# Two stacked transformer blocks on one core: the modulation weights multiplied in fp32 as they land, and a new order of the first weight units

## The reference

```python
mod = silu(c) @ w_ada + b_ada            # w_ada: 1024 x 6144
sh1, sc1, gt1, sh2, sc2, gt2 = split(mod, 6)
mod_c = silu(c_ctx) @ w_ada + b_ada      # the context's, first two parts used
h  = rmsnorm(x, g_norm1) * (1 + sc1) + sh1
hc = rmsnorm(ctx, g_norm1) * (1 + scc1) + shc1
cq, ckv, kpe, rq, rk, rv, rg = split_proj(h @ w_in)   # and the same of hc
```

## Time and profile before

| | us |
|---|---|
| median of 3 runs (lowest, highest) | 853.25 (853.14, 853.38) |
| span of the profiled execution | 852.2 |
| runs' median less that span | 1.05 |
| PE busy | 834.3 (98%) |
| DVE busy | 588.2 (69%) |
| ACT busy | 468.1 (55%) |
| read from HBM | 150.97 MB, 178 GB/s over the span |

### The profile page before, as it was taken

The page is one execution under the profiler, slowest core; times in us unless marked ns, Lnnn a source line. Parts: engine busy times, 40 slices in busy tenths (PEclk is TensorE's granted clock), DMA queues, the critical chain, the costliest instruction groups (busy, mean ns, idle before and its releaser), DMA issues. The chain is left out here.

```text
span 852.2 us, 12805 instructions
## 1 busy us (share of the span) xinstructions
PE 834.3 (98%) x4919; PEld 721.0 (85%) x4919; DVE 588.2 (69%) x917; ACT 468.1 (55%) x757; POOL 16.8 (2%) x24
## 2 busy tenths in 40 slices
PE   7999999999999999999999999999999999999997
PEld 5798888877899999987889977788977788888785
DVE  5885978787778777796767676577547655555444
ACT  6866364366366666563555684646545644444442
POOL 1001000000000000000000000010000000000000
PEclk9999999999999999999999999999999999999999
DMA  9973573165656666568758643244504666665541
GB/s 332 374 237 98 173 229 106 50 198 173 217 169 184 198 186 183 179 205 310 240 145 290 196 149 100 75 164 158 173 25 149 185 185 198 177 192 177 190 154 49
DMA packets 103667, 152.85 MB, mean 179 GB/s; under 512 B 6538, under 2 KB 55862, under 8 KB 103608
## 3 DMA queue, kind: packets, MB, share of 16 engines
q1 hardware_dynamic: 102296, 149.21, 54.5%
q10 hardware_dynamic: 1312, 2.83, 0.9%
HBM read 150.97 MB, written 1.05 MB: 178 GB/s over the span
## 5 line engine op out<-in xcount | busy, mean ns | idle before, releaser
L2087 DVE TENSOR_TENSOR w_lo<-raw,w_hi 128x1024 fp32r<-128x1024 f32 (+1 forms) x244 | 294.9, 1213 | 150.2 <-ACT w_hi L1521 149.4
L1521 ACT ACTIVATE w_hi<-raw 128x1024 fp32r<-128x1024 f32 (+1 forms) x244 | 254.5, 1050 | 201.2 <-PE bank L738 142.2
L736 PE MATMUL bank<-w_hi,hT_hi 128*128 128x512 f32 (+2 forms) x400 | 156.1, 390 | 1.3 <-DVE w_lo L2087 0.6
L738 PE MATMUL bank<-w_hi,hT_lo 128*128 128x512 f32 (+2 forms) x400 | 152.9, 382 | 0.0
L737 PE MATMUL bank<-w_lo,hT_hi 128*128 128x512 f32 (+2 forms) x400 | 152.6, 382 | 0.0
L839 PE MATMUL bank<-hT_hi,w_hi 128*128 128x256 f32 x512 | 145.0, 283 | 0.0
L840 PE MATMUL bank<-hT_lo,w_hi 128*128 128x256 f32 x512 | 144.9, 283 | 0.0
L841 PE MATMUL bank<-hT_hi,w_lo 128*128 128x256 f32 x512 | 144.9, 283 | 0.0
L840 PEld LDWEIGHTS bank<-hT_lo,w_hi 128*128 128x128 f32 x512 | 98.3, 192 | 0.0
L839 PEld LDWEIGHTS bank<-hT_hi,w_hi 128*128 128x128 f32 x512 | 98.3, 192 | 0.0
L841 PEld LDWEIGHTS bank<-hT_hi,w_lo 128*128 128x128 f32 x512 | 98.3, 192 | 0.0
(11 more groups left out here) (341 smaller groups left out, 1197.9 us busy)
## 6 DMA issues: line engine op xcount, KB each, us to landing
raw<-w_up_dram SPq DMA_DIRECT2D x132, 256.0 KB, 3.2
raw<-w_ada_dram SPq DMA_DIRECT2D x48, 512.0 KB, 4.7
raw<-w_down_dram SPq DMA_DIRECT2D x44, 512.0 KB, 4.1
raw<-w_in_dram SPq DMA_DIRECT2D x40, 512.0 KB, 4.6
raw<-w_gate_dram SPq DMA_DIRECT2D x44, 256.0 KB, 2.8
raw<-w_out_dram SPq DMA_DIRECT2D x16, 512.0 KB, 3.4
raw<-wk_x_dram SPq DMA_DIRECT2D x8, 512.0 KB, 4.7
raw<-wv_x_dram SPq DMA_DIRECT2D x8, 512.0 KB, 3.4
```

The costliest lines, as they stand in the source:

```text
L736: pe.matmul(o, xh, yh, start=first, stop=False, skip_group_check=skip)
L738: return pe.matmul(o, xl, yh, start=False, stop=last, skip_group_check=skip)
L1521: act.activation(unit_view(w_hi[n % NSPLIT], u), unit_view(raw[u % NRAW], u), ACT.Copy).then_inc(w_hi_ready, 1)
L2087: dve.tensor_tensor(unit_view(w_lo[n % NSPLIT], u), unit_view(raw[u % NRAW], u), unit_view(w_hi[n % NSPLIT], u).bitcast(F32), ALU.subtract ...
```

## The change

- The sixteen units of ada0 to ada3 are no longer split. PE multiplies them in plain fp32 straight from `raw` (`direct_unit`): `c_cols` holds silu(c) in column 0 and silu(c_ctx) in column 1 of 32 (the rest are zeros, written by POOL), and each unit is four matmuls of 256 columns, one for each K tile and half of the columns, each on another 32 columns of the array. The four partial sums lie at PSUM partitions 0, 32, 64 and 96; `sel_col` (four columns now) adds them in `ada_spread`, with two matmuls instead of four. `modrow` is half as wide.
- The chunks come in the order 0, 2, 1, 3, and cq0, rq0 and rq1 are loaded, split and multiplied among the units of ada1 (the new `EARLIER`). x is loaded after units 1 and 3, the context after the last unit of ada3.
- PE waits for the landing (`raw_landed`) instead of `unit_ready`; SP waits for `direct_used` or the filled bank. `by_dve` counts the units that DVE still does.
- Fillers: 24 instead of 17 at the start, 4 instead of 3 after a unit, 16 instead of 8 (now after ada1's first unit).
- ACT makes silu from the bank itself, and splits cq1 before it does pairs 2 and 3 of x.

```diff
-EARLIER = {"cq": (("cq", 0), ("rq", 0), ("rq", 1)),
-           "wout2_0": (("wv1", 0), ("wv1", 1)),
-           "wo0": (("wo0", 0), ("wo0", 1), ("wo1", 0))}
+EARLIER = {("ada1", 0): (("cq", 0),), ("ada1", 1): (("rq", 0),), ("ada1", 3): (("rq", 1),),
+           ("wout2_0", 0): (("wv1", 0), ("wv1", 1)),
+           ("wo0", 0): (("wo0", 0), ("wo0", 1), ("wo1", 0))}
-    ada(range(4))
+    ada((0, 2, 1, 3))
-BUSY = {"score": 8, "start": 17, "spread": 8, "ada": 3,  "ffnpre": 14, "gu0": 8}
+BUSY = {"score": 8, "start": 24, "spread": 16, "ada": 4, "ffnpre": 14, "gu0": 8}
...
+            def direct_unit(u):
+                name, k0, nk, cols, _ = units[u]
+                use = (name, 0)
+                pe.wait_ge(raw_landed[u % NRAW], landed[u])
+                w = unit_view(raw[u % NRAW], u).rearrange("p (k n) -> p k n", k=nk)
+                for kk in range(nk):
+                    for half in range(2):
+                        j = 32 * (2 * kk + half)
+                        ins = pe.matmul(ps(use)[j:j + 32, 0:TOK], c_cols[:, k0 + kk, :],
+                                        w[:, kk, half * TOK:(half + 1) * TOK],
+                                        start=u == first_unit[name], stop=u == last_unit[name])
+                if u == last_unit[name]:
+                    fill(ins, use)
+                else:
+                    ins.then_inc(direct_used, 1)
...
+            turn_vectors(0, 4)
+            for p, b in ((0, 0), (2, 1), (1, 6), (3, 7)):
+                claim((f"ada{p}", 0), b)
+            idle = ps(("ada3", 0))[:, 0:P]
+            keep_busy(idle, BUSY["start"])
+            pe.wait_ge(csilu_ready, 3)
+            for u in units_of["ada0"]:
+                direct_unit(u)
+                keep_busy(idle, BUSY["ada"])
+            turn_vectors(1, 5)
             pe.wait_ge(in_sel, 16)
+            ada_spread(0, 2)
+            for u in units_of["ada2"]:
+                direct_unit(u)
+                if u != last_unit["ada2"]:
+                    keep_busy(idle, BUSY["ada"])
+            turn("x1", None, range(2), (4, 5))
+            ada_spread(2, 3)
+            direct_unit(units_of["ada1"][0])
+            keep_busy(idle, BUSY["spread"])
...
+            next(cq)
+            for u in units_of["ada1"][1:3]:
+                direct_unit(u)
+            next(rq)
+            direct_unit(last_unit["ada1"])
+            next(rq)
+            turn("x1", None, range(2, 4), (4, 5))
+            ada_spread(1, 6)
+            for u in units_of["ada3"]:
+                direct_unit(u)
             ada_spread(3, 7)
...
-                    sp.wait_ge(unit_ready, u - NRAW + 1)
+                    v = u - NRAW
+                    if not direct[v]:
+                        sp.wait_ge(unit_ready, by_dve[v])
+                    elif v in ends:
+                        ready(sp, (units[v][0], 0))
+                    else:
+                        sp.wait_ge(direct_used, inner_direct[v])
...
-                    if u == (4, 6)[t]:
+                    if u == (1, 3)[t]:
                         sp.dma_start(res[:, t, :], a["x"][t * P:(t + 1) * P, :]).then_inc(in_x[t], 16)
-                if u == first_unit["rq"]:
+                if u == last_unit["ada3"]:
                     sp.dma_start(in_ctx[:, :, :], a["ctx"].rearrange("(t p) d -> p t d", p=P)).then_inc(in_ctxx, 16)
```

More of the change, by code:

```diff
@@ L77, in constants @@
     c[:, C_ID:C_ID + P] = np.eye(P)
-    c[[0, 32], C_SEL] = 1
-    c[[64, 96], C_SEL + 1] = 1
+    for tile in range(4):
+        for i in range(2):
+            c[32 * tile + i, C_SEL + 2 * (tile % 2) + i] = 1
     c[:, C_ONES:C_ONES + P] = 1
@@ L159, in ada @@
         for p in ps:
-            add(f"ada{p}", "sum" if p in SUMMED else "ada", a["w_ada"], 512 * p, 512)
-    ada(range(4))
+            add(f"ada{p}", "sum" if p in SUMMED else "direct", a["w_ada"], 512 * p, 512)
+    ada((0, 2, 1, 3))
     add("cq", "rows", a["w_in"], 0, 256, nk=4)
@@ L287, in build @@
     panels = plan_panels(a)
-    units, units_of, summed = [], {name: [] for name, *_ in panels}, []
+    units, units_of, summed, direct = [], {name: [] for name, *_ in panels}, [], []
     def add_unit(name, k0, nk, cols, sources, kind):
@@ L311, in build @@
     first_unit = {name: us[0] for name, us in units_of.items()}
[L313 removed]
+    split_units = [u for u in range(len(units)) if not summed[u] and not direct[u]]
     split_of = {u: n for n, u in enumerate(split_units)}
     ends = set(last_unit.values())
[L316 removed]
+    inner = np.cumsum([u not in ends and not summed[u] and not direct[u] for u in range(len(units))]).tolist()
+    by_dve = np.cumsum([not d for d in direct]).tolist()
+    inner_direct = np.cumsum([u not in ends and direct[u] for u in range(len(units))]).tolist()
+    landed, _count = {}, [0] * NRAW
+    for u, (_, _, _, _, sources) in enumerate(units):
+        _count[u % NRAW] += 16 * len(sources)
+        landed[u] = _count[u % NRAW]
     def reach(u, held=0):
@@ L941, in ada_spread @@
                 fill(ins, use)
-            for p in range(4):
-                claim((f"ada{p}", 0), p)
-            keep_busy(ps(("ada3", 0))[:, 0:P], BUSY["start"])
-            pe.wait_ge(c_lo_ready, 2)
-            def chunk_unit(chunk):
-                next(chunk)
-                keep_busy(ps(("ada3", 0))[:, 0:P], BUSY["ada"])
-            chunk = ada_steps(0)
-            for _ in range(4):
-                chunk_unit(chunk)
-            run(chunk)
-            chunk = ada_steps(1)
-            chunk_unit(chunk)
@@ L959, in _ @@
-            chunk_unit(chunk)
-            turn_vectors(1)
-            next(chunk)
-            pe.wait_ge(in_sel, 16)
-            ada_spread(0, 0)
-            run(chunk)
-            chunk = ada_steps(2)
-            next(chunk)
-            next(chunk)
-            ada_spread(1, 1)
-            next(chunk)
-            turn("x1", None, range(2))
-            run(chunk)
-            chunk = ada_steps(3)
-            next(chunk)
-            turn("x1", None, range(2, 4))
-            ada_spread(2, 2)
```

157 lines of the change are left out of this document (64 added, 93 removed).

## The result

| | before | after |
|---|---|---|
| median of runs (lowest, highest), first comparison | 853.28 (853.14, 853.38), 4 runs | 856.85 (855.80, 859.42), 4 runs |
| the same kernels again, beside e9 to e11 | 853.97 (853.04, 855.80), 26 runs | 857.32 (855.73, 858.81), 5 runs |
| span of the profiled execution | 852.2 | 854.0 |
| start of `turn("ctx")` in it | 49.12 | 50.61 |

The changed kernel is slower by some 0.4%: the ratio of its time to that of the kernel before is 1.0045, with a 95% interval of 1.0033 to 1.0056, and 1.0038 (1.0023 to 1.0053) in the second comparison. The prediction was 852.2 with a range to 856.2; the median lies outside it.

A forecast was written before the change was run, and what follows sets the result against it. The start was taken as bound by transfers, with PE and the ACT and DVE chain close behind. `turn("ctx")` at 48.1 instead of 49.12 gains 1.0: span 852.2 - 1.0 = 851.2, plus 1.05 around it, 852.2; range 849.6 to 856.2.

The forecast's parts named there:

- That the end follows `turn("ctx")`: PE runs without a pause from 37.52, so whatever comes earlier at 49.12 comes earlier at the end.
- rival 4: Further on in the kernel: DVE or a transfer takes over and the gain is lost; 853.2, chance 0.04.
- The transfers after: Landing of cq1, again the 24th transfer at 1.46 us each: taken as unchanged at 38.95.
- PE's own work: Direct units on PE: 0.43 us of matmuls, 0.1 for tile change, 0.33 for four fillers; 0.87 us a unit.
- The PE path: PE from ada0 to the last spread: cq0 at 23.8, gain on DVE at 39.0, with 1.0 us to spare.
- The vectors until 15.9: Ahead of ada2, small transfers queue behind eight large ones; PE stands still from about 12.5 to 15.9.
- The chain from landing to cq1: Through ACT and DVE: cq1 lands at 38.95, is split, and PE begins it at 43.5 instead of 46.24.
- The clock at cq1: After 5.3 us without work on PE, a low clock costs 1.7 us; cq1 ends at 48.1.
- The 1.05 us around it: Time outside the profiled span, added to the forecast span of 851.2 to give 852.2.
- Rival 2: Clock low earlier, in ada2's units and cq0, 1.7 us each time; cq1 at 45.9; 854.6, chance 0.12.
- Rival 3: Direct units' four tiles run only two at a time, 0.43 us a unit more; 856.3, chance 0.13.
- rival 1: Transfers keep the better rate, cq1 lands at 36.3 and the PE path decides; gain 2.0 to 2.7, 850.9, chance 0.34.

The follow-up runs named there:

- e9: e8 with the context's transfer behind cq1, `w_lo` of cq0 and cq1 one place earlier on DVE, and 25 fillers; 852.75 us, ratio 0.9989.
- e11: e8 with only the context's transfer moved behind cq1; 853.06 us, ratio 0.9986 to the kernel before.
- e1: The changed kernel with 52 fillers between the last spread and cq1; 856.42 us, ratio 1.0033 to the kernel before.
- e13: e10 with the context's scaled row on DVE ahead of the split of rq's third unit; 852.92 us, ratio 0.9984 to the kernel before.
- e5: The changed kernel with both halves of cq0 split ahead of the x1 turns; 857.12 us, ratio 1.0033 to the kernel before.
- e8: e7 with 30 fillers between the last spread and cq1; 853.59 us, ratio 0.9995 to the kernel before.
- e3: The changed kernel with two column tiles of 64, two matmuls on each, instead of four of 32; 860.89 us, ratio 1.0083 to the kernel before.
- e10: e9 without the fillers in ada2's units; 853.62 us, ratio 0.9993 to the kernel before.
- e6: e5 with 30 fillers between the last spread and cq1; 856.22 us, ratio 1.0029 to the kernel before.
- e12: The changed kernel again, unaltered, on the chip of e9 to e11; five runs from 855.73 to 858.81 us.
- e2: The changed kernel without the three groups of four fillers between ada2's units; 854.96 us, ratio 1.0013 to the kernel before.
- e4: The changed kernel's direct multiplication in the old order, four fillers after ada1's and ada3's units too, 20 after the last spread; 855.89 us, ratio 1.0021.
- e7: The changed kernel with the vector transfers issued by ACT behind its silus, not by SP; 854.30 us, ratio 1.0007 to the kernel before.

## Why the prediction was wrong, step by step

Two of the three signs that the prediction named for its own failure are in the profile: PE is in rq1 until 36.1 (the limit was 35), and the last spread comes at 39.96 (39.5). The third, a wait of over 1 us for the context's rows, is not: PE had no wait there.

- **That the end follows `turn("ctx")`: right.** Span less the start of `turn("ctx")` is 803.1 before, 803.4 after, and 803.2 to 803.6 in e1 to e13. Only 0.3 us are lost further on (rival 4).
- **The transfers after, "I take its landing as unchanged, 38.95": wrong, the step that failed.** It landed at 41.4. The order of transfers was right, and so was 1.46 us for each while there are issues. But SP issues only when a buffer is free, and from ada2 on that follows PE: the issues from 17.42 to 20.89 wait for ada2's units, and those behind them for the splits of cq0 and rq0 on DVE and the direct units behind cq0 on PE, which all follow the first half of x. The prediction named only the last of these waits ("PE frees its buffer at about 27.2", SP could issue at 29.45), gave it 5.8 us of room, and missed SP's wait from 21.26 to 24.99. e5 suggests that this hole alone was not the cause; e8, with PE earlier, that the whole chain was: cq1 at 39.73. An estimate by the table: cq0 at the forecast 23.8 and 15.5 us more would have had cq1 at 39.3, near the 38.95.
- **PE's own work, 0.87 us a unit: the multiplication right, the fillers wrong.** Four tiles at once take 0.43 us, as assumed (e3 against it). But a change between the tile shapes costs about 0.15 us, and four fillers in a unit take 0.58 us, not 0.33: they are 0.113 us each in a long row (e1), where 0.083 was taken, and the change back is the rest. The Trainium skill, "TensorEngine Tiling (Array Packing)", Key Properties, says that changing the tiling mode drains the engine, without a number; the 1.93 us of four units in a row against 4 x 0.58 agree.
- **The PE path: 1.9 us late from ada2 on.** ada2 was bound by PE behind the vectors and not by landings: done at 20.8, not 18.9. Of these 1.9 us, 1.3 are the dearer units and a start at 16.72 instead of 16.3. The other 0.6 are a slip inside the prediction: by its own 0.87 us, four units from 16.3 on are done at 16.3 + 3 x 0.87 + 0.54 = 19.5, not half a microsecond behind the landing at 18.4. So cq0 came at 25.71, not 23.8, and the gain column at 41.1, not 39.0, past the 1.0 us of slack that the prediction gave it. This lateness also pushed back SP's waits, so both terms fail for one reason. Their shares, as an estimate: with the landing at 38.95, `fbuf` on ACT would have begun 0.25 us after the instruction that makes the gain column (40.90; as in e9 and e10), at 41.15 instead of 42.41. The landing alone is thus about 1.25 of the 2.35 us by which cq1 began late, and PE's path the rest.
- **The vectors until 15.9: right** (16.11), as a time; PE waited 2.0 us and not 3.4, as its own work took longer. What was not priced as likely is what such a wait does to the clock in a part of the runs.
- **The chain from landing to cq1: right.** 4.4 us from 41.45 to 45.85, against 4.5. e9, with cq1 there at 38.6 and the full clock, has `turn("ctx")` at 47.43, where the prediction had 47.4 without the clock's price.
- **The clock at cq1: right in place, 1.9 us instead of 1.7** (2.9 us of work from 45.85 to 50.61). In e1 it was worth 0.5 us, as the rows of the context stood close behind. The rule weighed there, that transposes bring no full clock, falls again: 52 of them hold it at 1.00 in e1, where without them it fell to 0.50.
- **"The 1.05 us around it": wrong by 0.75.** In every execution of the later comparisons whose span is known, of either kernel, time less span was 1.8 us (1.75 to 1.89). The profiled execution of before was thus one of about 854.0, not of 853.25. The forecast of the median doesn't suffer by it, since it was the gain that was taken off; but half of the difference between the medians (3.6 us, against 1.8 between the spans) is in which executions were profiled.

The sum with the measured terms: 48.1 + 2.35 (cq1's start) + 0.15 (clock) = 50.6 for `turn("ctx")`, + 803.4 + 1.8 = 855.8, the profiled execution's time. The median is 1.05 us above it, by the executions with a lower mean clock; e5 and e6 show a stretch where the clock can fall. That it is the same stretch in the runs without a trace is argued, not shown.

Rival 2 (the clock low earlier, 854.6) is thus at most a part of the truth, the one in the slower runs. Its times for cq1 (45.9) and `turn("ctx")` (50.5) are those of the profiled execution (45.85 and 50.61), but by luck: the granted clock was 1.00 there until 42. Rival 3 is excluded, and rival 1's rate (389 GB/s) was reached only in stretches, as in 36 to 40.

## What to carry to other kernels

A queue that issues in order has one gate for each buffer it reuses; when the order of units changes, write down for every issue who frees its buffer and when, and follow the latest, for a landing is "unchanged" only if all gates are. Work taken off an engine that only fed PE buys nothing if it puts PE's own steps, fillers and waits ahead of the release of buffers. When a unit's cost is worked out, use it again for every row of units: a row is done half a microsecond behind its last landing only if PE is not behind already. And a wait of PE of about 2 us should be priced at what it costs in the bad runs, since the median holds them.

## What was not expected of the hardware

- Four 32-column tiles with fp32 data run fully at once: 8 records of 256 columns in 0.43 us (1.93 us for 32), where two tiles take 0.86 (3.67 us for 32 in e3).
- Fillers of 128 x 128 take 0.113 us each in a long row (5.87 us for 52), 0.145 each in fours between direct units, and 0.21 to 0.23 in the first row of all (5.00 us for 24 after, 3.89 for 17 before), though the granted clock is printed as 1.00 there: at the start of the program the pace tells more than that number.
- A wait of PE of 1.6 to 2.7 us lowered the granted clock in some executions and not in others, and its length doesn't tell in which: behind the vectors, 1.90 us (e1), 2.01 us (after) and 2.56 us (e12) did not; 1.60 us (e2), 1.93 us (e6), 2.18 us (e4) and 2.65 us (e5) did. Before ada1's first unit 1.66 us (e11) and 1.81 us (e7) did and 2.13 us (e10) did not. The Trainium skill, "TensorE: Matmul & The Clock Gate", Part 1, says of a kernel's start that the count of slow matmuls differs between runs of one kernel. Here the later stretches differ too: the changed kernel took 855.7 to 859.4 us at mean granted clocks of 0.995 down to 0.991.
- Left open: e13's runs lie on two levels (851.3 to 851.8, and 852.9 to 853.2) at nearly one mean clock (0.998 to 0.999, and 0.996 to 0.998), 1.4 us apart in the span too. e10's do so as well (852.1 to 852.3, and 853.6 to 853.9), so the median of either hangs on how many runs fell on each.
